# Moving the Z gate projection of a hybrid attention/SSD/mLSTM step from the attention steps to the projection block

## The chip, the cores and the metric

The kernel runs on one core of one Trainium2 chip. The metric is the device time of one execution in microseconds (us): the median of three runs of the kernel before is 3695.59 us (3692.9 to 3698.9). Everything is computed in 32-bit floats. Engines are named as in the profile: PE (TensorE; PEld is its weight load), DVE (VectorE), ACT (ScalarE), POOL (GpSimd), SP (SyncE, which here only issues DMAs).

## The reference, cut to what matters

Two layers with 128 context tokens and 1024 latent tokens (1152 in all), width 1024. Layer 0 (even) is touched, layer 1 and the rest are not:

```python
hs = modulate(x, norm_mix, shift, scale)          # (1152, 1024)
q, k, v, z, xbc, dt = split(hs @ w_in_even)       # q, k, v: 512 columns each; z: 1024 columns
y_na  = softmax(q k^T over the window + rpb, and all context keys) @ v     # 8 heads of 64
y_ssd = rmsnorm(ssd_scan(silu(conv(xbc)), dt) * silu(z), norm_g)           # z is used only here
x = x + gate * (concat(y_na, y_ssd) @ w_out_even)
```

The product for z does not depend on the attention and is not needed by it; z is needed only by the SSD stage behind it.

## The kernel before

The kernel is a list of blocks; in a block each engine has its own instruction stream, and a block ends when all its engines have ended. The blocks around the change are, in order:

1. **Norm block** (`norm_mixer`), which leaves the modulated activations in `HT` (`hk`, feature-major).
2. **Projection block** (from L605). PE computes 24 feature tiles for q and k (`feature_tile`, 128x384) and 9 token tiles for v (`token_tile`: 8 matmuls of 512 columns for 128 tokens). Among the tiles stand the products for the adaLN vectors (`mod_products`), whose weights DVE folds first (`mod_fold`). Tile i uses PSUM bank i % 7; ACT copies it out. The weights come in slots of 2 MB (`WR`, two places): slots 0 to 2 are q, k, v, slots 3 and 4 are the two halves of z, slots 5 to 7 are xbc. `feed` issues the load of a slot once the slot two before it is used up (`free_at`). SP also loads the adaLN weights here.
3. **Attention block** (from L702). SP loads the cached keys `kcT`, the cached values `vc` and, per head, the bias table `rpbT` (`bias_load`); POOL adds the column mask to the table. There are NA = 72 steps: 8 heads of 8 query tiles, then 8 short steps for the context tokens. In 32 of the 64 full steps a ninth half tile of keys is read ("nine": 704 columns in place of 640). Step n is: `scores(n)` on PE; `softmax_max(n)` on DVE (add the bias, copy the context part, maximum, negate); `probs(n)` on ACT (exp); `turn(n)` on PE (transposes); `take(n)` on ACT (copy to SBUF); `values(n)` on PE; `normalise(n)` on DVE (L827, L829).
4. **Turning block** (from L881): 36 transposes of the attention's output.
5. **Convolution block** (from L951), on slots 5 to 7, and behind it the SSD stage, which reads z back from DRAM (`z_spill`).

The order of PE in the attention block is written out by hand. In step n: half of a z tile's products are spread around the step, one 512-column product (`gate_product`) ahead of `scores(n+1)` and one ahead of `values(n-1)`. A z tile is 8 such products, so 144 of them fill all 72 steps; `gate_take` copies a finished tile on ACT and `gate_store` on SP writes it to DRAM.

Two places in PSUM matter. Scores of step n use banks 2*(n%2) and 2*(n%2)+1, and the values of step m are summed in columns 256 to 319 of bank 2*((m+1)%2)+1. So `scores(n)` waits until `normalise(n-3)` has read its sum:

```python
if n >= 3:
    pe.wait_ge(output_taken.sem, output_taken.at(n - 2))
```

DVE's own order is `softmax_max(n)` and then `normalise(n - 2)`, and `probs(n)` on ACT waits for both.

Of the kernel before, what the change touches and what calls it, by code (L numbers as in the profile page):

```python
# [9 lines left out]
ACT = mybir.ActivationFunctionType  # L10
# [3 lines left out]
P = 128  # L14
# [107 lines left out]
def hybrid_step(nc, xT, vec, consts, wmod, wslots, wff, wsmall, rpbT, kcT, vc, ssd0, mls0, yT, o_k, o_v, o_ssd, o_mls, o_m):  # L122
    ctx = ExitStack()
    with ctx:
# [3 lines left out]
        def count(name):  # L128
            return Count(ctx.enter_context(nc.semaphore(name)))
# [65 lines left out]
        mod_folded = count("mod_folded")  # L195
        mod_used = count("mod_used")
        mod_ready = count("mod_ready")
        o_done, o_taken = count("o_done"), count("o_taken")
        small_done = count("small_done")
        gate_act = count("gate_act")  # L200
        out_raw = [count(f"out_raw{n}") for n in range(4)]
# [98 lines left out]
        def feed(sp, upto):  # L300

            while fed[0] < upto:
                n = fed[0]
                if n in free_at:
                    sp.wait_ge(*free_at.pop(n))
                sp.dma_start(WR[:, n % 2, :], wslots[n, :, :]).then_inc(w_ready[n % 2].sem, 16)
                fed[0] += 1

        def landed(n):

            return w_ready[n % 2].sem, 16 * (n // 2 + (1 if n < S_OUTE else 0))
# [222 lines left out]
        def slot_k(n):  # L534
            return WR[:, n % 2, :].rearrange("p (k n) -> p k n", k=KD)

        def frees(slots, per_slot):

            at = 0
            for n, k in zip(slots, per_slot):  # L540
                at += k
                free_at[n + 2] = (tile_done.sem, tile_done.at(at))

        def close_tiles(n):
            tile_done.close(n)
            tile_free.close(n)

        zst = MI[:, 0:2048].rearrange("p (s n) -> p s n", s=4)

        def gate_product(pe, q, s0, banks):
            i, k = q // KD, q % KD
            s, t = i // NT, i % NT
            if k == 0:
                if t == 0:
                    pe.wait_ge(*landed(s0 + s))
                if i >= 2:
                    pe.wait_ge(o_taken.sem, o_taken.at(i - 1))
            mm = nc.tensor.matmul(PS[:, banks[i % 2], :], hk[:, k, t * P:(t + 1) * P], slot_k(s0 + s)[:, k, :],  # L560
                                  start=(k == 0), stop=(k == KD - 1))
            if k == KD - 1:
                mm.then_inc(o_done.sem, 1)

        def gate_take(act, i, banks):
            act.wait_ge(o_done.sem, o_done.at(i + 1))
            if i >= 4:
                act.wait_ge(z_stage[i % 4].sem, z_stage[i % 4].at(16 * (i // 4)))
            act.activation(zst[:, i % 4, :], PS[:, banks[i % 2], :], ACT.Copy).then_inc(o_taken.sem, 1)

        def gate_store(sp, i):
            s, t = i // NT, i % NT
            sp.wait_ge(o_taken.sem, o_taken.at(i + 1))
            sp.dma_start(z_spill[t, :, s * 512:(s + 1) * 512], zst[:, i % 4, :]).then_inc(z_stage[i % 4].sem, 16)
# [5 lines left out]
        def close_gate():  # L580
            for n in range(4):
                z_stage[n].close(16 * len(range(n, 18, 4)))
            o_done.close(18)
            o_taken.close(18)

        def norm_mixer(l, upto):
# [11 lines left out]
        vtok = F1[:, 0:4608].rearrange("p (t n) -> p t n", t=NT)  # L598

        mod_place = [F1[:, 4608:8704], XT[:, 0:4096], XT[:, 4096:8192]]  # L600
        frees(range(S_QKV, S_Z), (12, 12, 9))
        for s in range(2):
            free_at[S_Z + 2 + s] = (o_done.sem, o_done.at(NT * (s + 1)))

        with nc.Block() as block:  # L605
            @block.sync
            def _(sp):
                def mod_load(n):
                    sp.dma_start(mod_place[(n - 4) % 3], wmod[n, :, :]).then_inc(mod_loaded[(n - 4) % 3].sem, 16)

                mod_load(4)
                mod_load(5)
                mod_load(6)
                for n in range(7, NMOD):
                    if n in (12, 20):
                        feed(sp, S_Z if n == 12 else S_Z + 1)
                    sp.wait_ge(mod_folded.sem, n - 2)
                    mod_load(n)
                feed(sp, S_XBC)

            @block.tensor
            def _(pe):
                i, n = 0, 4
                for s in range(3):
                    pe.wait_ge(*landed(S_QKV + s))
                    for j in range(12 if s < 2 else NT):
                        if s < 2:
                            feature_tile(pe, i, slot_k(S_QKV + s), (j // NC) * P, j % NC, banks=7)
                        else:
                            token_tile(pe, i, slot_k(S_QKV + s), j, banks=7)  # L630
                        i += 1
                        if n < NMOD and 2 * i >= 8 + 3 * (n - 4):
                            mod_products(pe, n, mod_place[(n - 4) % 3], KD)
                            n += 1
                assert n == NMOD

            @block.scalar
            def _(act):
                n = 4
                for i in range(33):  # L640
                    if n < NMOD and 2 * i >= 3 * (n - 4):
                        place = mod_loaded[(n - 4) % 3]
                        act.wait_ge(place.sem, place.at(16 * ((n - 4) // 3 + 1)))
                        mod_begin(act, n, mod_place[(n - 4) % 3])
                        n += 1
                    act.wait_ge(tile_done.sem, tile_done.at(i + 1))
                    s, b, c = i // 12, i % 12 // NC, i % NC
                    if s < 2:
                        act.activation((qT, kT)[s][:, b, c * TC:(c + 1) * TC], PS[:, i % 7, 0:TC], ACT.Copy,
                                       scale=(HD ** -0.5, 1.0)[s]).then_inc(tile_free.sem, 1)  # L650
                    else:
                        act.activation(vtok[:, i - 24, :], PS[:, i % 7, :], ACT.Copy).then_inc(tile_free.sem, 1)
                assert n == NMOD

            @block.vector
            def _(dve):
                for n in range(4, NMOD):
                    place = mod_loaded[(n - 4) % 3]
                    dve.wait_ge(place.sem, place.at(16 * ((n - 4) // 3 + 1)))
                    mod_fold(dve, n, mod_place[(n - 4) % 3], KD)  # L660
                dve.wait_ge(mod_used.sem, NMOD)
                mod_values(dve, 0, 16, 48)
                mod_values(dve, 1, 0, 48)
                for l, n in ((0, 1), (1, 0), (1, 1)):
                    mod_gains(dve, l, n)
        close_tiles(33)


        T2 = F1[:, 4608:6400].rearrange("p (s r c) -> p s r c", s=2, r=14)
# [32 lines left out]
        with nc.Block() as block:  # L702
            @block.sync
            def _(sp):
                sp.dma_start(kcT_sb, kcT).then_inc(loaded.sem, 16)
                sp.dma_start(vc_sb, vc).then_inc(loaded.sem, 16)
                sp.dma_start(o_k, kT[:, :, 0:P]).then_inc(stored.sem, 16)
                sp.dma_start(o_v, vtok[:, 0, :]).then_inc(stored.sem, 16)

                def bias_load(h):  # L710
                    if h >= 2:
                        sp.wait_ge(scores_taken.sem, scores_taken.at(8 * (h - 1)))
                        sp.wait_ge(bias_ready.sem, bias_ready.at(h - 1))
                    sp.dma_start(T2[:, h % 2, :, :], rpbT[h]).then_inc(bias_loaded[h % 2].sem, 16)

                bias_load(0)
                bias_load(1)
                for i in range(2 * NT):
                    if i >= 2 and i % 2 == 0 and i // 2 + 1 < NH:
                        bias_load(i // 2 + 1)  # L720
                    gate_store(sp, i)
                gate_stored(sp)
                feed(sp, S_XBC + 2)
                sp.wait_ge(stored.sem, stored.at(32))

            @block.gpsimd
# [17 lines left out]
            def _(pe):  # L744
# [40 lines left out]

                scores(0)
                for n in range(NA):
                    gate_product(pe, 2 * n, S_Z, (6, 7))
                    if n + 1 < NA:
                        scores(n + 1)  # L790
                    turn(n)
                    gate_product(pe, 2 * n + 1, S_Z, (6, 7))
                    if n >= 1:
                        values(n - 1)
                values(NA - 1)
# [44 lines left out]
            def _(act):  # L840
# [23 lines left out]
                for n in range(1, NA):  # L864
                    take(n - 1)
                    probs(n)
                    if n % 4 == 0:
                        gate_take(act, n // 4 - 1, (6, 7))
                take(NA - 1)
                gate_take(act, 2 * NT - 1, (6, 7))  # L870
        loaded.close(32)
        stored.close(32)
        close_gate()
# [2019 lines left out]
```

## Time and profile before

| | |
|---|---|
| median of three runs | 3695.59 us (3692.9 to 3698.9) |
| the profiled execution | 3704.6 us, of which the span of the trace is 3702.8 us |
| PE busy | 3449.5 us (93% of the span) |
| DVE busy | 2058.7 us (56%) |
| ACT busy | 943.9 us (25%) |
| POOL busy | 579.3 us (16%) |
| projection block, PE's last work | ends at 323.1 us |
| attention block, first to last DVE work | 336.4 to 692.5 us |
| turning block, first transpose | 695.5 us |
| convolution block, first matmul | 703.7 us |

The table's first two lines say that the profiled execution is 9.0 us longer than the median. The times of blocks are read from the trace's order of time; they count from the start of the span. An engine's busy share is a mean over stages, so it doesn't say what bounds one stage.

### The profile page before, as it was taken

How to read it: one execution, taken by the hardware profiler on the slowest of the kernel's cores; microseconds unless marked ns; L12 is line 12 of the kernel's file. 1: busy time of each engine (PE TensorE's matmuls, PEld its weight loads, DVE VectorE, ACT ScalarE, POOL GpSimd, SP SyncE). 2: the span in 40 equal slices, each digit the busy share in tenths (PEclk: the TensorE clock that was granted, in tenths of full speed). 3: DMA queues.
4: the chain of work that ended last, by engine and by line, in shares of the span. 5: the costliest groups of instructions: out<-in, count | busy, mean ns of one | idle time of the engine just before them, and what ended most of it. 6: DMA issues, size and time to landing. Idle time of an engine off the chain costs nothing. (4 is left out here: it accounts for less than half of the span.)

```text
span 3702.8 us, 47736 instructions
## 1 busy us (share of the span) xinstructions
PE 3449.5 (93%) x18499; PEld 2981.9 (81%) x18499; DVE 2058.7 (56%) x3570; ACT 943.9 (25%) x1812; POOL 579.3 (16%) x510
## 2 busy tenths in 40 slices
PE   4998999999786999999999979999987999999997
PEld 3664666565453899999999968888887999999996
DVE  4894444223797475555444467655447555554446
ACT  3222333212123343111222124222234211122211
POOL 0000000000774131111111100322222111011110
PEclk9999999999897999999999989999998999999999
DMA  5661000100002331111111121222142111111111
GB/s 198 232 261 54 22 30 17 57 23 1 23 1 111 108 111 41 46 40 34 45 45 45 40 80 31 76 63 61 51 122 92 40 46 40 41 39 45 45 40 57
DMA packets 156324, 236.49 MB, mean 64 GB/s; under 512 B 8172, under 2 KB 129684, under 8 KB 151820
## 3 DMA queue, kind: packets, MB, share of 16 engines
q1 hardware_dynamic: 156172, 234.41, 18.8%
q8 instruction: 102, 1.67, 0.2%
q14 instruction: 50, 0.41, 0.0%
HBM read 217.75 MB, written 16.63 MB: 63 GB/s over the span
## 5 line engine op out<-in xcount | busy, mean ns | idle before, releaser
L1535 PE MATMUL PS<-AHL,WH 128*128 128x384 f32 x3072 | 783.4, 336 | 6.0 <-DVE WL L1803 6.0
L1535 PE MATMUL PS<-Y,WH 128*128 128x384 f32 x3072 | 780.6, 335 | 3.1 <-issue 3.1
L1823 DVE SCALAR_TENSOR_TENSOR XT<-PS,MOD,XT 128x384 f32<-128x384 f32 (+2 forms) x1024 | 495.3, 514 | 224.8 <-PE PS L1535 224.7
L1535 PEld LDWEIGHTS PS<-AHL,WH 128*128 128x128 f32 x3072 | 557.2, 189 | 6.6 <-DVE WL L1803 6.6
L1535 PEld LDWEIGHTS PS<-Y,WH 128*128 128x128 f32 x3072 | 554.6, 188 | 4.2 <-issue 3.7
L1535 PE MATMUL PS<-AHL,WL 128*128 128x384 f32 x1536 | 515.3, 335 | 0.0
L1535 PE MATMUL PS<-Y,WL 128*128 128x384 f32 x1536 | 513.7, 334 | 0.0
L1810 DVE TENSOR_TENSOR AHL<-SQ,AHL 128x384 fp32r<-128x384 f32 x192 | 157.8, 822 | 433.5 <-ACT AHL L1636 433.5
L1737 POOL TENSOR_TENSOR SQ<-RT 128x384 f32<-128x384 f32 x192 | 180.0, 937 | 1319.4 <-ACT RT L1631 1300.0
L523 PE MATMUL PS<-HT,WR 128*128 128x384 f32 x960 | 319.0, 492 | 14.7 <-PEq L429 13.5
L1625 ACT ACTIVATE WH<-WU 128x1024 fp32r<-128x1024 f32 x128 | 135.5, 1059 | 726.0 <-DMA WU<-in_wff 726.0
L523 PEld LDWEIGHTS PS<-HT,WR 128*128 128x128 f32 x960 | 182.8, 193 | 137.8 <-issue 19.3
L1535 PEld LDWEIGHTS PS<-AHL,WL 128*128 128x128 f32 x1536 | 289.9, 189 | 0.0
L1535 PEld LDWEIGHTS PS<-Y,WL 128*128 128x128 f32 x1536 | 288.4, 188 | 0.0
L1803 DVE TENSOR_TENSOR WL<-WU,WH 128x1024 fp32r<-128x1024 f32 x128 | 156.4, 1223 | 122.9 <-ACT WH L1625 119.9
L1631 ACT ACTIVATE RT<-PS 128x384 f32<-128x384 f32 x192 | 93.8, 488 | 438.3 <-PE PS L1535 438.3
L1520 PE MATMUL PS<-Y,OW 128*128 128x384 f32 x864 | 153.3, 338 | 6.1 <-DVE OW L1751 6.1
L2232 PE MATMUL PS<-Y,PH 128*128 128x384 f32 x576 | 151.7, 344 | 7.4 <-ACT XT L2385 4.2
L1520 PEld LDWEIGHTS PS<-Y,OW 128*128 128x128 f32 x864 | 151.8, 190 | 7.2 <-DVE OW L1751 6.6
L560 PE MATMUL PS<-WR,HT 128*128 128x512 f32 x288 | 154.8, 620 | 0.0
L1520 PE MATMUL PS<-Y,OWO 128*128 128x384 f32 x576 | 109.6, 353 | 24.2 <-DVE Y L1849 18.4
L358 DVE SCALAR_TENSOR_TENSOR MI<-XT,SM,MI 128x512 f32<-128x512 f32 x182 | 122.6, 747 | 12.3 <-ACT MI L346 11.8
(325 smaller groups left out, 4772.2 us busy)
## 6 DMA issues: line engine op xcount, KB each, us to landing
WU<-in_wff SPq DMA_DIRECT2D x128, 512.0 KB, 3.5
XT<-in_wmod SPq DMA_DIRECT2D x13, 2048.0 KB, 7.8
F<-in_wmod SPq DMA_DIRECT2D x9, 2048.0 KB, 8.0
OWR<-in_wslots SPq DMA_DIRECT2D x24, 768.0 KB, 5.1
WR<-in_wslots SPq DMA_DIRECT2D x8, 2048.0 KB, 8.7
PW<-in_wslots SPq DMA_DIRECT2D x24, 512.0 KB, 4.8
OWOR<-in_wslots SPq DMA_DIRECT2D x24, 512.0 KB, 4.3
EX<-b_rows SPq DMA_DIRECT2D x72, 128.0 KB, 3.2
```

What stands on the lines that cost most here:

```text
L358: ins = nc.vector.scalar_tensor_tensor(out=f, in0=w[:, k, :], scalar=g, in1=f, op0=ALU.mult, op1=ALU.add)
L523: mm = nc.tensor.matmul(PS[0:m, i % banks, 0:n], lhs, rhs, start=(t == 0), stop=(t == len(terms) - 1))
L560: mm = nc.tensor.matmul(PS[:, banks[i % 2], :], hk[:, k, t * P:(t + 1) * P], slot_k(s0 + s)[:, k, :], start=(k == 0), stop=(k == KD - 1))
L1520: mm = nc.tensor.matmul(PS[:, 3 + n % 4, 0:TC], w, y, start=(k == 0 and i == 0), stop=(k == kk - 1 and i == 2))
L1535: mm = nc.tensor.matmul(out, wt(w), x, start=(n == 0 and i == 0), stop=(n == len(terms) - 1 and i == 2))
L1625: act.activation(WH[place][:, :], WU[place][:, :], ACT.Copy).then_inc(unit_hi.sem, 1)
L1631: act.activation(RT2[:, j % 2, :], PS[:, j % 3, 0:TC], ACT.Relu).then_inc(up_taken.sem, 1)
L1737: nc.gpsimd.tensor_tensor(SQ2[:, j % 2, :], RT2[:, j % 2, :], RT2[:, j % 2, :], ALU.mult)\
L1803: nc.vector.tensor_tensor(WL[place][:, :], WU[place][:, :], WH[place][:, :].bitcast(F32), ALU.subtract).then_inc(unit_split.sem, 1)
L1810: nc.vector.tensor_tensor(AHL[:, g % 2, 1, m, t], SQ2[:, j % 2, :], AHL[:, g % 2, 0, m, t].bitcast(F32), ALU.subtract).then_inc(hidden_spl ...
L1823: ins = nc.vector.scalar_tensor_tensor(out=x, in0=PS[:, 3 + j % 4, a - c * TC:e - c * TC], scalar=MOD[:, l, 40 + b, cond:cond + 1], in1=x, ...
L2232: mm = nc.tensor.matmul(PS[:, bank, 0:TC], w[s][:, k * P:(k + 1) * P], h(c, k), start=(k == 0 and n == 0), stop=(k == KD - 1 and n == 2))
```

## The change

The two z slots are treated as two more slots of nine token tiles each in the projection block. PE's loop there has five slots in place of three (51 tiles in place of 33). ACT's loop copies the 18 new tiles into the four staging places `zst`, which move to the upper half of `MI` because the folds use the lower one, and SP stores them to DRAM at the end of its stream, before it feeds slots 5 and 6. In the attention block `gate_product` and `gate_take` are gone, and SP only loads the bias tables. The counter `o_done` and both helpers are deleted.

```diff
-        frees(range(S_QKV, S_Z), (12, 12, 9))
-        for s in range(2):
-            free_at[S_Z + 2 + s] = (o_done.sem, o_done.at(NT * (s + 1)))
+        frees(range(S_QKV, S_Z + 2), (12, 12, 9, 9, 9))
@@ projection block, SP
                 feed(sp, S_XBC)
+                for i in range(2 * NT):
+                    gate_store(sp, i)
+                gate_stored(sp)
+                feed(sp, S_XBC + 2)
@@ PE
-                for s in range(3):
+                for s in range(5):
@@ ACT
-                for i in range(33):
+                for i in range(51):
...
-                    if s < 2:
+                    if i >= 33:
+                        z = i - 33
+                        if z >= 4:
+                            act.wait_ge(z_stage[z % 4].sem, z_stage[z % 4].at(16 * (z // 4)))
+                        act.activation(zst[:, z % 4, :], PS[:, i % 7, :], ACT.Copy).then_inc(o_taken.sem, 1)
+                        act.wait_ge(o_taken.sem, o_taken.at(z + 1))
+                        act.sem_inc(tile_free.sem, 1)
+                    elif s < 2:
@@ attention block, SP
-                for i in range(2 * NT):
-                    if i >= 2 and i % 2 == 0 and i // 2 + 1 < NH:
-                        bias_load(i // 2 + 1)
-                    gate_store(sp, i)
-                gate_stored(sp)
-                feed(sp, S_XBC + 2)
+                for h in range(2, NH):
+                    bias_load(h)
@@ PE
                 for n in range(NA):
-                    gate_product(pe, 2 * n, S_Z, (6, 7))
                     if n + 1 < NA:
                         scores(n + 1)
                     turn(n)
-                    gate_product(pe, 2 * n + 1, S_Z, (6, 7))
                     if n >= 1:
                         values(n - 1)
@@ ACT
                     take(n - 1)
                     probs(n)
-                    if n % 4 == 0:
-                        gate_take(act, n // 4 - 1, (6, 7))
                 take(NA - 1)
-                gate_take(act, 2 * NT - 1, (6, 7))
```

## Rows read from the trace of the kernel before

**Rows 1.** Long stretches: length, busy time of PE, PEld, DVE, ACT, POOL, PEclk, DMA share, GB/s
```profile
999.00:1131.00 132.00, 117.50 (x525) 69.98 (x524) 127.25 (x89) 26.27 (x44) 95.41 (x34) 1.00 0.00 1
350.00:660.00 310.00, 310.00 (x1529) 198.47 (x1528) 149.99 (x389) 113.91 (x285) 18.20 (x24) 1.00 0.07 22
330.00:343.00 13.00, 10.45 (x18) 4.97 (x19) 3.82 (x8) 2.49 (x6) 6.05 (x8) 0.50 0.28 106
```
**Rows 2.** PE in order of time: V tiles, fold products, first scores. Columns: start, length (us)
```profile
307.42 13.98 PE L523 MATMUL PS<-WR,HT 128*128 128x512 f32 x32
321.24 1.84 PE L373 MATMUL PS<-CO,MI 128*128 128x1 f32 x16
330.52 2.07 PE L760 MATMUL PS<-F 64*128 64x512 f32 x2 [7.44 <-DMA F<-in_vc]
```
**Rows 3.** A full step of 640 columns, all engines in order of time
```profile
453.43 1.12 PE L760 MATMUL PS<-F 64*128 64x512 f32 x2
453.79 0.19 ACT L846 ACTIVATION_READ_ACCUMULATOR XT<-XT 128x1 f32 x1
...
454.70 0.77 PE L772 MATMUL PS<-CO,XT 128*128 128x128 f32 x5
454.81 0.69 DVE L812 TENSOR_TENSOR XT<-PS,F 128x512 f32<-128x512 f32 x1 [1.85 <-PE PS L761]
...
455.31 1.02 PE L560 MATMUL PS<-WR,HT 128*128 128x512 f32 x2
...
456.17 1.59 PE L782 MATMUL PS<-F,XT 128*128 128x64 f32 x12
...
456.72 0.15 DVE L821 TENSOR_SCALAR XT<-XT 128x1 f32<-128x1 f32 x1
...
457.68 1.12 PE L560 MATMUL PS<-WR,HT 128*128 128x512 f32 x2
457.79 0.16 DVE L827 RECIPROCAL XT<-XT 128x1 f32<-128x1 f32 x1 [0.92 <-PE PS L782]
...
458.37 0.83 ACT L846 ACTIVATE XT<-XT 128x640 f32<-128x640 f32 x1 [2.10 <-DVE XT L829]
...
458.74 1.12 PE L760 MATMUL PS<-F 64*128 64x512 f32 x2
```
**Rows 4.** First scores matmul of a 704-column step, PE
```profile
468.35 1.12 PE L760 MATMUL PS<-F 64*128 64x512 f32 x2
```
**Rows 5.** The same 704-column step on DVE
```profile
469.90 0.69 DVE L812 TENSOR_TENSOR XT<-PS,F 128x512 f32<-128x512 f32 x1 [1.87 <-PE PS L763]
...
472.00 0.15 DVE L821 TENSOR_SCALAR XT<-XT 128x1 f32<-128x1 f32 x1
```
**Rows 6.** A short step for context tokens, PE and DVE in order of time
```profile
674.25 0.49 PE L755 MATMUL PS<-F 64*128 64x128 f32 x2
...
674.77 0.29 DVE L807 COPY XT<-PS 128x128 f32<-128x128 f32 x1 [0.85 <-PE PS L755]
...
675.42 0.15 DVE L821 TENSOR_SCALAR XT<-XT 128x1 f32<-128x1 f32 x1
```
**Rows 7.** SP's last slot load ahead of the attention block
```profile
321.44 0.33 SPq L306 DMA_DIRECT2D WR<-in_wslots  x1
```
**Rows 8.** DVE's first work in the attention block
```profile
336.42 0.69 DVE L812 TENSOR_TENSOR XT<-PS,F 128x512 f32<-128x512 f32 x1 [12.06 <-POOLq L741]
```
**Rows 9.** The end of the attention block, engines in order of time
```profile
690.44 1.02 PE L560 MATMUL PS<-WR,HT 128*128 128x512 f32 x2
...
692.26 0.28 DVE L829 TENSOR_SCALAR XT<-PS,XT 128x64 f32<-128x64 f32 x1
694.20 0.81 SPq L306 DMA_DIRECT2D WR<-in_wslots  x2
695.51 7.00 PE L888 MATMUL PS<-CO,XT 128*128 128x128 f32 x36 [3.65 <-PEq L702]
```
**Rows 10.** Two slot loads in flight, columns as in rows 1
```profile
698.00:700.00 2.00, 2.00 (x11) 2.00 (x10) 0.00 (x0) 1.27 (x3) 0.00 (x0) 0.50 0.99 422
```

## What the change should do to the time

> **What bounds the kernel now.** I read the profile in this order: the long stretches with each engine's busy time, to find which engine is full around the change; the order of time inside one attention step, to see who waits for whom; then the two ends of the attention block, where DMAs decide.
>
> In the attention block PE is busy 310.00 of 310 us at full clock, DVE 149.99 and ACT 113.91 [rows 1]. So PE alone sets the length of a step, and every other engine waits for it: DVE sits idle 1.85 us ahead of its first add and 0.92 us ahead of the normalisation [rows 3]. Two of PE's pieces in each step are z products: one starts at 455.31 and the next piece at 456.17 (0.86 us), the other starts at 457.68 and the next scores at 458.74 (1.06 us) [rows 3]. The reader should see two things: a z product costs PE about 0.96 us, and nothing else in the step needs it. It fills time in which DVE and ACT work.
>
> In the projection block PE is full too: the last two V tiles stand back to back, from 307.42 to 321.24 [rows 2], 13.82 us for two, 6.91 us each.
>
> So the work is moved from one place where PE is full to another where PE is full. The 18 tiles must cost the same or a little less there. The question is what a step of the attention costs without them: it can't shrink below the chain that the other engines form.
>
> **Part 1: the 18 z tiles in the projection block.** They are the same instructions as the V tiles (8 products of 512 columns; another slot). 18 x 6.91 = 124.4 us [rows 2], all on PE and all on the path, since PE is the last engine there (the folds on DVE and their last products, which end at 321.24 + 1.84 = 323.08, stay in front of them). ACT's copy of one tile per 6.91 us, the store and the wait for a staging place are hidden under the tiles; with seven banks PE doesn't wait for copies. Slot 3 is loaded early as before; slot 4 is issued when the V tiles end, as before (321.44) [rows 7], and now has nine tiles, 62 us, to land. Uncovered it would show as PE idle ahead of the tenth z tile; cost 0.
>
> **Part 2: a step of the attention without its z products.** What is late next? `scores(n+1)` waits until `normalise(n-2)` has read the bank, and DVE reaches `normalise(n-2)` only after `softmax_max(n)`, which needs `scores(n)`. That is a closed loop, once per step:
> - scores to DVE's first add: 453.43 to 454.81, 1.38 us [rows 3]; with 704 columns 468.35 to 469.90, 1.55 us [rows 4, 5];
> - first add to the end of the negation: 454.81 to 456.87, 2.06 us [rows 3]; with 704 columns 469.90 to 472.15, 2.25 us [rows 5];
> - normalisation and the release of the waiting engine: 457.79 to 458.37, 0.58 us [rows 3].
>
> Sum 4.02 us, with 704 columns 4.38; half of the 64 full steps are of each kind, so 4.2 us. The rest must fit inside. PE behind the scores: transposes from 454.70, 0.77 us, then values of at most 1.59 us [rows 3]: they end 2.36 us after 454.70, against DVE's 2.17; since successive pieces overlap by some 0.15 us (0.77 long, 0.61 apart) the two come out level. ACT: from the normalisation's release 0.83 for the exp, then the read of its sum, 0.19 [rows 3], 1.0 us, while the scores take 1.38; fits. In the kernel before the z products hide this loop (4.2 below the PE's own step, which is 3.39 us without and 5.31 with z products from 453.43 to 458.74 [rows 3]). Who is queued behind the wait of the scores: on PE the transposes and values of the same step, and DVE's next add.
>
> 64 steps at 4.2. How many of them at the start are slow is a second term: PE's clock was at half speed when the block began (0.50 from 330 to 343, a score matmul pair 2.07 us in place of 1.12) [rows 1 to 3], and will be again. For the first four scores I take 12 us from DVE's first add (bounds 9 and 17: four fast steps less the lead, or two cold ones). Then 60 x 4.2 = 252. The 8 short steps have the same loop: 0.52 (674.25 to 674.77) + 0.80 (to 675.57) [rows 6] + 0.58 = 1.9 us, 15 us. The drain after the last scores, 3 us, is an estimate from the same pieces (0.8 DVE, 0.5 exp, 1.2 transposes, copy and values, 0.5 DVE). Sum 282 to 283 us from DVE's first add to its last end. Before it was 336.42 to 692.54 [rows 8, 9], 356.1. **Saved: 73 us.**
>
> **Part 3: the way into the attention.** Before, DVE's first add stood 336.42 - 323.08 = 13.3 us after PE's last projection work [rows 2, 8]; it waits for the masked bias table. SP now passes three more things there: the last z store, the wait for its landing, and the loads of slots 5 and 6, all ahead of the keys, values and bias tables. From the end of the last z product to the slot loads: 690.44 + 1.02 to 694.20, 2.7 us [rows 9]. From the last slot load to the first add: 321.44 to 336.42, 15.0 us [rows 7, 8], with one slot ahead of the small loads. Now there are two; 2.1 MB more at 422 GB/s [rows 10] is 5.0 us. Together 22.7 in place of 13.3: **+9.3 us**. Bounds: 0 if the small loads pass the slots in the queue; 12 if both slots land later than this. I take 9.3, because the first scores waited 7.44 us for the values with one slot in front [rows 2].
>
> **Part 4: the way out.** No store and no slot loads stand at the end: SP's 2.7 us go. Last DVE work 692.54 to first transpose 695.51 is 3.0 us [rows 9]; about 0.5 of it is the crossing between blocks: **-2.5 us** (bounds 0 and -4, the latter if the 36 transposes of 7.00 us also run partly at a higher clock). The bias loads no longer queue behind stores on SP; POOL has a head's time in hand (18 us of work in 310 [rows 1]): 0.
>
> **Sum against the profiled execution:** 3704.6 + 124.4 + 9.3 - 73 - 2.5 = 3762.8. The median of the runs is 9.0 below the profiled one: **3754 us**, 1.6% slower.
>
> **Rival A, the steps shrink to PE's own length; not slower.** If the loop doesn't bind (the release of the bank comes early enough, so that the z products were pure PE time), a step takes 3.39 us or, with fewer value records, less: 3.3. Attention 12 + 60 x 3.3 + 15 + 3 = 228, saved 128; net +3 us, 3699, and with the handover at its bound 0 about 3690. It decides from a step at or under 3.35 us. For it speaks that DVE's busy time, 149.99 us in 58 to 60 steps, is only 2.5 a step [rows 1]; against it, that DVE's work lies in series with the scores, and the wait is written in the code. Chance 5%.
>
> **Rival B, PE's clock falls inside the steps.** A step has 3.39 us of PE work in 4.2, and its gaps return in each step. At half clock PE's chain decides: scores, transposes and values at about 1.85 times their length (2.07 against 1.12 [rows 2, 3]), 1.38 + 0.61 + 1.5 becoming 6.4, with 0.58 for the normalisation 6.9 us a step, 2.7 more. With three in ten steps cold +50 us, 3805; all of them +165, 3920. For it: in the first 13 us of the block PE worked 10.45 us and the clock stayed at 0.50 [rows 1]. Against it: a later stage holds clock 1.00 for 132 us with PE busy 117.50 (89%) in the same pattern of waits on DVE [rows 1]; here it would be some 80%. The Trainium skill (TensorE: Matmul & The Clock Gate, section "A second HAM failure mode: psum-queue depth-cycling") says that short idles between matmul groups, coming back with each turn of the PSUM banks, can make the clock swing; its Part 4 adds that transposes don't count as activity. By these rules this rival is the outcome; the 132 us are the row that speaks against them, with a busier PE. Chance 17%.
>
> **Rival C, waits cost more than the rows show.** PE hardly waits inside a step before, so its restart after a wait and the level race of values against DVE could add 0.3 to 0.5 us a step: 4.6 us, +19 to +32, 3773 to 3786. Chance 12%.
>
> **How the numbers follow.** Forecast 66%: 3754; its own range is 3736 (handover 0, way out -4, a step of 4.1) to 3773 (first scores 17, handover 12, a step of 4.35). Range 3733 to 3805: the low end leaves out rival A, the high end the worse half of rival B, together some 15 to 20%. A measurement of this kernel tells about 0.2% (7 us) from no change. Slower by more: forecast, B and C, 95%; within: most of A, 4%; faster: A with the handover at 0, 1%.
>
> **What would show it.** Right: z tiles 6.9 us apart; a period of the full steps of 4.0 to 4.4 us at clock 1.00; PE's longest total wait in the block ahead of the scores (L760), released by DVE's normalisation (L829); DVE without a long idle ahead of L827; first add some 22 us after the last z tile; the turning block 3 us after the last scores' drain. Wrong: PE near 100% busy between the steps (rival A), a PEclk under 0.95 in the middle of the block (B), periods of 4.6 with idle time that ends at other releasers (C), or PE idle between z tiles.

## The result and the profile after

The changed kernel takes 3933.72 us (median of 4 executions, 3928.58 to 3934.75) against 3696.45 us for the kernel before on the same chip: ratio 1.064, 95% interval 1.0621 to 1.0658. It is 237 us slower; the forecast was 58 us slower, and its range ended at 3805. Ratios here leave out executions whose mean clock lay below that of the same kernel's others, for which there is no trace: one of 29 of the kernel before (3997 us, mean clock 0.83) and three of ten of e8_half below (3934 to 3943 us, 0.91).

The page of the profile cuts the span into 40 slices of 98 us. For the kernel after, the rows give the busy tenths of PE and of DVE and PE's granted clock in tenths of full speed.

```profile
PE   4999799998988959999999997999997999999997
...
DVE  5891033332247965545555446766546545555456
...
PEclk9999855557999979999999998999998999999999
```

The clock is at 5 tenths in four slices, and PE's row shows 9 above each of them: PE is "busy" and runs at half speed. These slices are the attention block. The order of time shows its way in, against [rows 2, 7, 8] of before:

```profile
440.03 0.60 ACT L634 ACTIVATE MI<-PS 128x512 f32<-128x512 f32 x1 [6.27 <-PE PS L523]
446.90 0.60 ACT L634 ACTIVATE MI<-PS 128x512 f32<-128x512 f32 x1 [6.27 <-PE PS L523]
449.58 0.81 SPq L306 DMA_DIRECT2D WR<-in_wslots  x2
```

```profile
464.04 2.07 PE L745 MATMUL PS<-F 64*128 64x512 f32 x2 [17.18 <-DMA F<-in_vc]
```

```profile
469.97 0.69 DVE L795 TENSOR_TENSOR XT<-PS,F 128x512 f32<-128x512 f32 x1 [145.54 <-POOLq L726]
```

The z tiles are 6.87 us apart (440.03 to 446.90). The last one's product ends at 446.86 (464.04 less the 17.18 that PE waits for the cached values), the two slot loads leave at 449.58, and DVE's first add stands at 469.97: 133.6 us later than before, 23.1 us behind the last z product.

A steady step, for [rows 3 to 5]; first the stretch of 400 us with busy times, PEclk, DMA share and GB/s in the last columns, to be read against [rows 1]:

```profile
500.00:900.00 400.00, 361.98 (x1233) 279.25 (x1232) 143.21 (x372) 102.87 (x260) 18.20 (x24) 0.50 0.02 7
```

```profile
648.93 2.04 PE L745 MATMUL PS<-F 64*128 64x512 f32 x2 [0.67 <-DVE XT L812]
...
651.65 1.54 PE L757 MATMUL PS<-CO,XT 128*128 128x128 f32 x6
651.75 0.69 DVE L795 TENSOR_TENSOR XT<-PS,F 128x512 f32<-128x512 f32 x1 [2.97 <-PE PS L748]
...
652.99 2.23 PE L767 MATMUL PS<-F,XT 128*128 128x64 f32 x10
...
653.86 0.15 DVE L804 TENSOR_SCALAR XT<-XT 128x1 f32<-128x1 f32 x1
...
655.25 0.16 DVE L810 RECIPROCAL XT<-XT 128x1 f32<-128x1 f32 x1 [1.24 <-PE PS L767]
...
655.88 2.04 PE L745 MATMUL PS<-F 64*128 64x512 f32 x2 [0.67 <-DVE XT L812]
```

6.95 us from scores to scores (648.93 to 655.88); 57 normalisations in the 400 us make 7.0 us a step. PE's pieces are 1.7 to 1.8 times as long as at full clock: the pair of scores 2.04 in place of 1.12 [rows 3], six transposes 1.54 in place of 0.87 and ten value records 2.23 in place of 1.23 (both from the first steps of e1, below). The order is the predicted one: the next scores wait for DVE's L812, the normalisation. But DVE is not what makes it late: it idles 1.24 us for PE's values (the RECIPROCAL at 655.25). At half clock the loop runs through PE: scores, transposes, values, normalisation.

The way out, for [rows 9]; the last DVE work of the block ends at 933.41:

```profile
933.13 0.28 DVE L812 TENSOR_SCALAR XT<-PS,XT 128x64 f32<-128x64 f32 x1
```

```profile
933.74 5.68 PE L868 MATMUL PS<-CO,XT 128*128 128x128 f32 x36 [0.84 <-PEq L691]
940.80 9.59 PE L523 MATMUL PS<-HT,WR 128*128 128x384 f32 x29 [1.39 <-PEq L861]
```

From last DVE work to the convolution's first matmul 7.4 us, before 11.2 (692.54 to 703.70). So the 237 us are: first add 133.6 later, attention 463.4 us (469.97 to 933.41) in place of 356.1, which is +107.3, and the way out -3.8. Sum +237.1.

That this sum meets the difference of the medians is partly luck. The two profiled executions are 229.6 us apart (3934.2 less 3704.6): behind the convolution's first matmul the one of before took 2999.1 us (703.7 to 3702.8) and the one of after 2991.6 (940.8 to 3932.4), in stages that the change doesn't touch. The forecast had allowed for it with its 9.0 us between the profiled execution and the median.

### The profile page after: what moved, and what is told of

It is laid out like the page before. It is cut to its first block and busy times, and to the rows that moved or that the text cites. A ratio compares the mean times of both kernels' runs of the same rounds, so it can differ in the third digit from the quotient of the medians.

```text
span 3932.4 us, 47755 instructions
## 1 busy us (share of the span) xinstructions
PE 3624.9 (92%) x18499; PEld 3127.5 (80%) x18499; DVE 2057.5 (52%) x3570; ACT 946.4 (24%) x1812; POOL 578.9 (15%) x510
## 5 line engine op out<-in xcount | busy, mean ns | idle before, releaser
L795 DVE TENSOR_TENSOR XT<-PS,F 128x512 f32<-128x512 f32 x64 | 44.3, 692 | 320.4 <-POOLq L726 145.5
L523 PE MATMUL PS<-WR,HT 128*128 128x512 f32 x432 | 187.1, 593 | 0.0
L745 PE MATMUL PS<-F 64*128 64x512 f32 x128 | 130.5, 1122 | 57.9 <-DVE XT L812 40.7
L767 PEld LDWEIGHTS PS<-F,XT 128*128 128x128 f32 x720 | 164.9, 331 | 5.3 <-ACT XT L838 0.2
L767 PE MATMUL PS<-F,XT 128*128 128x64 f32 x720 | 166.9, 412 | 0.0
L523 PEld LDWEIGHTS PS<-WR,HT 128*128 128x128 f32 x432 | 81.5, 190 | 100.0 <-issue 100.0
```

The lines of the kernel that those rows point to most:

```text
L523: mm = nc.tensor.matmul(PS[0:m, i % banks, 0:n], lhs, rhs, start=(t == 0), stop=(t == len(terms) - 1))
L745: nc.tensor.matmul(PS[:, b, :], q, kT[r, h // 2, k0:k0 + 512], start=True, stop=True)
L767: mm = nc.tensor.matmul(PS[:, 2 * ((n + 1) % 2) + 1, 256:256 + HD], PT[0:m, n % 2, i * P:(i + 1) * P], v, start=(i == 0), stop=(i == len(c ...
L795: nc.vector.tensor_tensor(s[:, 0:512], PS[:, b, :], bias[:, 0:512], ALU.add).then_inc(dve_own.sem, dve_own.one())
```

## The experiments

What was open after the result: does the clock fall because PE has gaps (waits on DVE), because the block is entered at half clock after 17 us of idle time, or because the steps hold too little work; and what would the loop be at full clock. All kernels but the last are the changed kernel with an edit or two. "Filler" is a product of PE into a PSUM bank that nobody reads; it changes no output. Ratios are against the kernel before, measured beside each of them.

**e1_warm_entry**: full clock at the entry, nothing added in the steps.

```diff
+                def filler(cols=512):
+                    nc.tensor.matmul(PS[:, 6, 0:cols], ident, hk[:, 0, 0:cols], start=True, stop=True)
+                for _ in range(12):
+                    filler()
                 scores(0)
...
+                    if n == 0:
+                        for _ in range(8):
+                            filler()
                     turn(n)
```

> The changed kernel with 20 idle-time products of 512 columns on PE into an unused bank, 12 ahead of the first scores and 8 ahead of the first transposes, so that the steps are entered at full clock. Theory 'entry' (the clock is only not brought back after the 17 us gap; once high it stays): steps of 4.2 us at PEclk 1.00, attention near 285 us, total near 3755. Theory 'level' (the steps without z products hold too little work for full clock at any time): PEclk falls to 0.50 within the first tens of us, steps of 6.95 us, total within 10 us of 3934.

Measured: 3922.85 us, ratio 1.0609 (1.0578 to 1.064). Three stretches and the steps in them; the columns are those of [rows 1]:

```profile
471.00:481.00 10.00, 8.70 (x52) 6.27 (x50) 6.42 (x17) 5.15 (x13) 1.03 (x4) 1.00 0.01 2
481.00:491.00 10.00, 8.01 (x50) 6.34 (x51) 5.63 (x17) 4.40 (x11) 0.00 (x0) 1.00 0.00 1
491.00:501.00 10.00, 9.33 (x39) 7.40 (x37) 4.36 (x10) 2.95 (x9) 0.00 (x0) 0.56 0.04 9
```

```profile
475.33 1.23 PE L767 MATMUL PS<-F,XT 128*128 128x64 f32 x10
477.34 1.09 PE L745 MATMUL PS<-F 64*128 64x512 f32 x2 [0.78 <-DVE XT L820]
...
478.76 0.87 PE L757 MATMUL PS<-CO,XT 128*128 128x128 f32 x6
...
481.66 1.09 PE L745 MATMUL PS<-F 64*128 64x512 f32 x2 [0.96 <-DVE XT L820]
...
486.04 1.09 PE L745 MATMUL PS<-F 64*128 64x512 f32 x2 [0.67 <-DVE XT L820]
...
490.43 1.09 PE L745 MATMUL PS<-F 64*128 64x512 f32 x2 [0.67 <-DVE XT L820]
...
496.06 2.04 PE L745 MATMUL PS<-F 64*128 64x512 f32 x2 [0.67 <-DVE XT L820]
```

For the first steps the clock is 1.00 and the period 4.32 to 4.39 us (477.34, 481.66, 486.04, 490.43), three periods of 704-column steps: the loop was forecast at 4.38. The scores' wait is released by the normalisation (L820 in this kernel). Then, with PE busy 8.0 of 10 us, the clock falls, and from there a step takes 7.0 us (50 normalisations in 350 us). The theory "entry" alone is out: these steps don't keep full clock. With PE busy 80% at full clock they come out just as the forecast had them ("some 80%").

**e2_product_filler**: one filler of 512 columns ahead of the scores in each step.

```diff
                 for n in range(NA):
+                    filler()
                     if n + 1 < NA:
                         scores(n + 1)
```

> The changed kernel with one idle-time product of 512 columns per step, ahead of the scores, into an unused bank: 72 products, 62 us of PE work at full clock if none is hidden. Theory 'level': the added work brings the clock back to 1.00, steps of 4.3 to 4.5 us, total near 3765, so more work gives less time. Theory 'gaps' (the clock stays low since PE waits on DVE once a step): PE still waits, clock 0.50, steps of 8 to 8.5 us, total near 4020.

Measured: 3765.29 us, ratio 1.0183 (1.0153 to 1.0212). Useless work of some 62 us (72 fillers at the 0.86 us of a z product [rows 3], an estimate) took 168 us off the changed kernel. The block is entered at half clock, as in the changed kernel, and the clock comes back between 470 and 480:

```profile
450.00:470.00 20.00, 6.45 (x9) 2.65 (x10) 0.53 (x1) 1.17 (x1) 3.53 (x5) 0.53 0.76 297
470.00:480.00 10.00, 7.79 (x34) 4.72 (x33) 5.80 (x15) 3.54 (x9) 2.53 (x4) 0.74 0.00 0
480.00:500.00 20.00, 19.95 (x111) 13.61 (x110) 10.61 (x28) 8.19 (x22) 0.00 (x0) 1.00 0.00 1
500.00:550.00 50.00, 49.64 (x269) 33.36 (x269) 28.57 (x77) 20.43 (x51) 6.09 (x8) 1.00 0.06 19
```

**e3_transpose_filler**: the same place, 8 transposes of 128 columns.

```diff
+                def filler():
+                    for i in range(8):
+                        nc.tensor.transpose(PS[:, 6, (i % 4) * P:(i % 4) * P + P], hk[:, i, 0:P], ident)
...
                 for n in range(NA):
+                    filler()
```

> As the kernel with one product of 512 columns per step, but with 8 transposes of 128 columns there, about as long on PE (0.85 us at full clock, 1.7 at half). If the clock goes by PE's busy time, the result is that of the product filler (near 3765). If transposes don't count for it, the clock stays at 0.50, steps of 8 to 8.5 us, total near 4020.

Measured: 3764.50 us, ratio 1.0181 (1.0151 to 1.021), clock 1.00 in the steps:

```profile
500.00:720.00 220.00, 218.36 (x1491) 176.26 (x1491) 123.95 (x329) 90.56 (x227) 18.30 (x24) 1.00 0.05 14
```

The Trainium skill (TensorE: Matmul & The Clock Gate, Part 4) says that full clock doesn't engage for transposes, since they don't count as busy in the same way. This run doesn't bear that out for these 32-bit transposes: as filler they did what products did, 3764.50 against 3765.29 us.

**e4_own_banks**: the loop opened. The values are summed in banks 6 and 7, so the scores don't wait for the normalisation.

```diff
-                    if n >= 3:
-                        pe.wait_ge(output_taken.sem, output_taken.at(n - 2))
...
-PS[:, 2 * ((n + 1) % 2) + 1, 256:256 + HD]
+PS[:, 6 + n % 2, 0:HD]
```

> The changed kernel with the values summed in banks 6 and 7, which the z tiles left free, so that the scores no longer wait for the normalisation two steps back. Theory 'gaps': PE no longer waits, the clock rises, steps of 3.4 to 3.6 us, attention near 240 us, total near 3710. Theory 'level': PE is busy all the time at half clock (6.3 us a step) with the same work a step; whether that is enough is what this run tells; if not, total near 3890.

Measured: 3877.45 us, ratio 1.0486 (1.0456 to 1.0517).

```profile
500.00:850.00 350.00, 350.00 (x1237) 271.64 (x1237) 143.47 (x373) 102.93 (x259) 18.23 (x24) 0.50 0.03 8
```

PE is busy 350.00 of 350 us by the trace's records and the clock stays at 0.50; a step takes 6.0 us (58 in 350). Opening the loop gave 56 us, but the theory "gaps" is out as the reason why the clock stays low: without any gap it doesn't come back.

**e6_small_filler**: the filler of e2 with 256 columns.

> The changed kernel with an idle-time product of 256 columns per step, half of the filler that brought the clock back (0.43 us of PE at full clock). If that is still enough: clock 1.00, steps of 4.3 us, total 3752 to 3760. If not: clock 0.50, steps near 7.6 us, total near 3975; the clock then makes a step of 200 us between two fillers that differ by 0.43 us a step.

Measured: 3958.52 us, ratio 1.0704 (1.0682 to 1.0725), with PE full, the clock low and 7.3 us a step (48 in 350):

```profile
500.00:850.00 350.00, 350.00 (x1126) 255.45 (x1125) 120.22 (x312) 84.93 (x215) 18.17 (x24) 0.50 0.03 8
```

Half the filler costs 193 us more than the whole one.

**e9_small_filler_warm**: the 256-column filler in the steps and the 20 products of e1 at the entry.

```diff
+                for _ in range(12):
+                    filler()
                 scores(0)
                 for n in range(NA):
+                    filler(256)
...
+                    if n == 0:
+                        for _ in range(8):
+                            filler()
```

> The 256-column filler per step, which left the clock at 0.50, now with the 20 idle-time products at the entry that bring the first steps to full clock. Theory 'level alone decides': clock falls again, total near 3950. Theory 'two states' (at full clock the same steps hold more work per us than at half clock, so the clock that a block is entered with is kept): 1.00 throughout, steps of 4.3 us, total near 3752.

Measured: 3755.89 us, ratio 1.0165 (1.0145 to 1.0185).

```profile
500.00:720.00 220.00, 206.67 (x1236) 153.92 (x1234) 128.95 (x341) 93.51 (x235) 18.23 (x24) 1.00 0.04 14
```

The steps of this kernel and of the one above are the same instructions; they run at 0.50 or at 1.00 throughout, by the clock with which the block is entered. 20 products at the entry are worth 203 us. This is also the check of the forecast's loop over the whole block, since the small filler lies in time in which PE waits: 4.2 us a step (52 in 220), 285.4 us from DVE's first add to its last work (471.62 to 757.03) in place of the forecast's 282 to 283, and a total 2 us from the forecast's 3754. Only the clock was missing.

**e10_own_banks_warm**: e4 with the 20 products at the entry (into bank 5). Its steps hold the same work as those of e1, without the wait for the normalisation.

> The changed kernel with the values in banks of their own and the 20 idle-time products at the entry. At full clock its steps should be 3.4 to 3.6 us with PE nearly full, the densest steps that this work allows. Theory 'two states': clock 1.00 throughout, attention near 240 us, total 3690 to 3710. Theory 'level alone decides, and this work is too little at any speed': falls within tens of us, total near 3870.

Measured: 3730.68 us in the profiled execution, 3789.45 in the other one, whose mean clock was 0.951 in place of 0.972. In the profiled one the clock holds through the full steps and falls in the short ones behind them:

```profile
500.00:700.00 200.00, 178.31 (x1164) 139.59 (x1162) 134.81 (x353) 96.68 (x244) 18.19 (x24) 1.00 0.04 13
700.00:720.00 20.00, 15.28 (x87) 12.47 (x85) 10.19 (x36) 8.20 (x25) 0.00 (x0) 0.77 0.00 1
```

```profile
560.40 0.77 PE L755 MATMUL PS<-CO,XT 128*128 128x128 f32 x5 [0.67 <-ACT XT L835]
```

Even this one missed the expected 3690 to 3710: a step takes 3.7 us (54 in 200) in place of 3.4 to 3.6, since PE still waits up to 0.7 us a step for the exp on ACT.

The other lost it for part of the block, I suppose; there is no trace of it. With e4 (0.50 throughout) the one trace shows that these steps can run at either clock. And with e1 it shows that the smaller work of a step alone doesn't bring the clock down: e1's steps hold the same work, were entered at full clock too, and fell.

**e11_own_banks_early**: e4, and keys, values and two bias tables loaded and masked ahead of the z tiles; the slot loads moved into the attention block. No filler.

```diff
                     mod_load(n)
+                sp.wait_ge(mod_folded.sem, NMOD - 1)
+                sp.dma_start(kcT_sb, kcT).then_inc(loaded.sem, 16)
+                sp.dma_start(vc_sb, vc).then_inc(loaded.sem, 16)
+                for h in range(2):
+                    sp.dma_start(T2[:, h, :, :], rpbT[h]).then_inc(bias_loaded[h].sem, 16)
+            @block.gpsimd
+            def _(pool):
+                mask(pool, 0)
+                mask(pool, 1)
```

> The changed kernel with own banks for the values and with keys, values and two bias tables loaded and masked ahead of the z tiles, so that PE goes from the z tiles into the attention with a gap of about 2 us in place of 17, with no filler. If the state at the entry is kept: total near 3690, or 3680 if steps come out at 3.4. If the short gap already drops the clock, as it did for 7 us in the kernel before with early loads, and nothing brings it back: near 3860.

Measured: 3859.05 us, ratio 1.0445 (1.0428 to 1.0463). PE enters at full clock (scores 1.09 us) and loses it within 6 us:

```profile
448.00 1.09 PE L753 MATMUL PS<-F 64*128 64x512 f32 x2 [1.42 <-PEq L603]
...
452.42 1.33 PE L765 MATMUL PS<-CO,XT 128*128 128x128 f32 x5 [2.02 <-ACT XT L837]
453.68 2.07 PE L753 MATMUL PS<-F 64*128 64x512 f32 x2
```

The first transposes wait 2.02 us for the first exp, since no earlier step is there to fill the time; the scores behind them already take 2.07. Nothing brings the clock back: from 500 to 850 it is 0.50.

**e5_small_first**: the changed kernel with SP's slot loads behind the small loads.

```diff
                 gate_stored(sp)
-                feed(sp, S_XBC + 2)
...
+                feed(sp, S_XBC + 2)
                 for h in range(2, NH):
                     bias_load(h)
```

> The changed kernel with SP's two slot loads issued after the keys, values and first two bias tables instead of ahead of them. If the 17.2 us that PE waits for the values is the queue of the two slots, DVE's first add comes 9 to 10 us earlier (17 us after the last z tile in place of 23) and nothing else moves: clock still 0.50 in the steps, total near 3924. If the small loads weren't held up by the slots, 3934.

Measured: 3923.66 us, ratio 1.0609; PE's wait for the values is 6.50 us and DVE's first add comes 9.4 us earlier:

```profile
453.57 2.07 PE L745 MATMUL PS<-F 64*128 64x512 f32 x2 [6.50 <-DMA F<-in_vc]
...
460.55 0.69 DVE L795 TENSOR_TENSOR XT<-PS,F 128x512 f32<-128x512 f32 x1 [135.91 <-POOLq L726]
```

The reason for the late start is confirmed: the small loads stood behind the two slots. The run doesn't separate the term's parts (store and second slot). The first scores still take 2.07 us.

**e8_half**: nine z tiles in the projection block, nine left in the attention with one product a step.

```diff
-                for s in range(5):
+                for s in range(4):
...
                 for n in range(NA):
+                    half_product(pe, n)
                     if n + 1 < NA:
                         scores(n + 1)
```

> Half of the change: the first nine z tiles in the projection block, the other nine left in the attention steps with one product a step (where the product filler stood). Theory: the clock needs the added work in the steps and not its being idle work, so PEclk 1.00, steps of 4.45 us as with the filler, and the total is that of the product filler (3765) less 9 tiles of 6.9 us: 3703. Rival (the change costs by itself what it moves, half of 237 us): 3815.

Measured: 3706.02 us as the median of ten executions. Seven took 3695.5 to 3706.4 (median 3703.09, ratio 1.0013, 1.0002 to 1.0024), and the trace of one of them has clock 1.00 in the steps:

```profile
500.00:600.00 100.00, 99.38 (x539) 66.94 (x537) 55.80 (x151) 42.03 (x105) 9.14 (x12) 1.00 0.07 22
```

There half of the change costs next to nothing, as expected (3703). The other three took 3934 to 3943 us, as long as the whole change: with half of the z products in the steps, most executions kept a high mean clock (0.97) and some didn't (0.91).

**e7_early_loads**: the kernel before, with the early loads and masks of e11, and the wait for the last z store moved into the turning block.

> The kernel before with the z products left in the steps, but keys, values and the first two bias tables loaded, and the tables masked on POOL, while the last folds run, and the wait for the last z store moved one block on. If the 13.3 us from PE's last projection work to DVE's first add are that queue of loads, about 9 of them go, with some 4 to 6 us of half clock behind them and 2 us at the end: total 3678 to 3684. If the start of the block is bound by something else, 3694 to 3697.

Measured: 3686.84 us, ratio 0.9964 (0.9951 to 0.9976), the shortest of all. The first two scores, and DVE's first add:

```profile
324.31 1.09 PE L769 MATMUL PS<-F 64*128 64x512 f32 x2 [1.59 <-PEq L625]
...
327.56 2.07 PE L769 MATMUL PS<-F 64*128 64x512 f32 x2
```

```profile
325.66 0.69 DVE L821 TENSOR_TENSOR XT<-PS,F 128x512 f32<-128x512 f32 x1 [1.67 <-PE PS L770]
```

The first add comes 10.8 us earlier than [rows 8] (about 9 were expected), and the total gains 11 us (median before 3698.06), short of the 14 to 20 expected. The clock is high at the entry (scores 1.09 us) and still falls for some steps: the scores at 327.56 take 2.07 us. Slow steps at the start remain, only earlier.

## Why the prediction was wrong

Point by point, forecast against measured:

- 18 z tiles: 124.4 us, 6.91 each. Measured 6.87 each. Right.
- The way in: first add 22.7 us behind the last z product, 133.7 later in all. Measured 23.1 and 133.6. Right, and e5 shows that the small loads' place behind the two slots is the reason.
- The way out: -2.5 with a bound of -4. Measured -3.8; the 36 transposes took 5.68 in place of 7.00 us.
- The loop that bounds a step: scores, softmax, normalisation, scores; 4.38 us for 704 columns at full clock. In the first steps of e1, at full clock: 4.32 to 4.39. Over both kinds of step the forecast was 4.2, and e9, at full clock throughout, has 4.2. Right.
- The clock in the steps: this step of the forecast failed. The sum took all but the first four of the 64 full steps at full clock. They ran at half, 7.0 us each (rival B priced 6.9 and, for all steps cold, 3920 us; measured 3934). The mechanism and its price stood on the record with 17% beside the forecast's 66%, the range cut off its full form, and the likeliest case was the wrong one. 64 steps at 7.0 in place of 4.2 are 179 us: the whole difference between 3754 and 3934.
- The arithmetic: two slips, neither of weight. B's own terms, 3.49 us at 1.85 and 0.58, give 7.0 us, the step that was measured, and not 6.9. The ends of the forecast's own range come to 3737 and 3771 by its terms, not 3736 and 3773.

What misled was how the evidence on the clock was read. The row for it was a later stage at clock 1.00 with PE busy 89% [rows 1], while the forecast expected some 80% here. At full clock e1 had that 80% (8.01 of 10 us) and fell; e10 with 89% (178.31 of 200) and e9 with 94% (206.67 of 220) held. So the row didn't cover the case. The shares can't be compared across clocks either: the changed kernel's steps have 90.5% (361.98 of 400) at clock 0.50, e4 and e6 have 100% at 0.50. At half clock PE's pieces are 1.7 to 1.8 times as long, so PE looks busy because it is slow. Another row was already there: in 13 us at the block's start, with the z products still in the steps, PE was busy 10.45 us and the clock was at 0.50 [rows 1]. The steps before had to climb back from half clock, and the change took two of PE's longest products out of them.

What the runs put in its place: with the work of the kernel before the steps climb back to full clock, and with that of the changed one they don't; between the two lie steps that stay at the clock at which they are entered. At 256 filler columns a step (e6, e9) the same steps run at 0.50 or 1.00 by the entry, and so, in the one trace of it, does the changed kernel's work with its loop opened (e4, e10). With 512 more columns they climb back (e2, e3, and e8 in seven of ten executions). With the loop closed and no filler (e1) they fall even from full clock. There either remedy was enough to hold it: filler in the idle time (e9, same period of 4.2 us) or the same work in 3.7 us (e10). Both make PE's idle share smaller, so whether the length of the single idle pieces or their sum counts is not told apart. At half clock e4 shows that gaps are not what keeps it low.

Rival A (steps at PE's own length) was wrong: the loop exists, in e1's waits and in the 56 us that e4 gained by opening it. Rival C is out: e1's steps show no extra cost of the waits. The claim that the z products cost PE 0.96 us that nothing else needs was the deepest error: useless products in their place (e2) bring the clock back to 1.00, so the z products did that too.

## What to carry to other kernels

Work that fills PE between dependent small matmuls can be what holds its clock; before moving it, ask at which clock the remaining step would run, entered at either clock, and price both. At a low PEclk don't read PE's busy share as load: compare the length of one known matmul (here a pair of scores, 1.1 or 2.0 us). Issue a block's small loads ahead of its large ones: that gained 10 us in e5 and 11 in e7. It gained the wait alone; the clock was low in the first steps all the same (e5, e7, e11), and only products in the idle time kept it up there (e1, e9).

## What the runs showed of the hardware that was not expected

PE busy without a gap, by the trace's records, for 350 us at a granted clock of 0.50 (1.2 GHz), with no rise (e4, e6). The same instructions at 0.50 throughout or at 1.00 (2.4 GHz) throughout, by 20 products ahead of them: 3958.5 against 3755.9 us (e6, e9). From full clock, steps with the same work fell within some 20 us with PE busy 80% (e1) and held for 200 us with 89% (e10, one trace). Transposes as filler were as good as products: 3764.5 against 3765.3 us (e3, e2).
